# A sink bias added on VectorE, and a normalization issued in two stages, in a two-layer encoder

## What is computed

```
qkv = h @ w_qkv                       # 16 query heads, 4 key/value heads of 64
scores = q k^T / 8 - slope * |t - s|  # only |t - s| <= 128
den = sum exp(scores - m);  lse = m + log(den)
o = (exp(scores - m) @ v) / den
o = o * sigmoid(lse - sink)           # one learned sink logit for each head
x = x + o @ w_out
```

## Time and profile before

| | |
|---|---|
| Runs | 5187.29, 5196.99 and 5769.88 us; median 5196.99 |
| Profiled execution | 5184.39 us; span of its slowest core 5183.3 us |
| Spans of the 8 cores | 5171.3 to 5183.3 us, granted clock 0.932 to 0.936 |
| Busy share of the span | PE 88%, DVE 42%, ACT 27%, POOL 5% |
| DMA | 160.19 MB, mean 31 GB/s |

### The profile page before, as it was taken

How to read it: one execution, slowest core, us unless ns; L and a number is a source line. 1 busy time by engine, 2 the same in 40 slices (tenths; PEclk the granted TensorE clock), 3 DMA queues, 4 the chain that set the end, 5 groups by cost and what they waited for, 6 DMA issues and landing times.

```text
span 5183.3 us, 77281 instructions; the slowest of 8 cores (5171.3 to 5183.3 us)
## 1 busy us (share of the span) xinstructions
PE 4538.4 (88%) x27104; PEld 2251.7 (43%) x27104; DVE 2187.1 (42%) x3136; ACT 1397.6 (27%) x2762; POOL 246.4 (5%) x471
## 2 busy tenths in 40 slices
PE   5767999999999998999767679998999999979996
PEld 2333344455554543444323333443554545434442
DVE  4322322355656565322342233224556565662223
ACT  1574201222232223211215733012132222231112
POOL 0000100000000000000000001000000000000000
PEclk9888899999999998999878889998999999989997
DMA  4100322111111111222221004221111111122211
GB/s 90 25 1 1 56 37 39 21 22 23 21 21 24 19 24 22 41 39 39 58 85 25 1 1 60 37 39 17 26 19 23 21 22 24 23 29 33 39 23 65
DMA packets 85013, 160.19 MB, mean 31 GB/s; under 512 B 8864, under 2 KB 8864, under 8 KB 84640
## 3 DMA queue, kind: packets, MB, share of 16 engines
q0 software_dynamic: 66816, 121.66, 16.5%
q1 hardware_dynamic: 17824, 33.58, 2.1%
HBM read 260.07 MB, written 16.78 MB: 53 GB/s over the span
## 4 chain that ended last, share of the span: by engine, by line
PE 80%; ACT 9%; DVE 5%; issue 4%; DMA 2%; ACTq 0%; DVEq 0%; SPq 0%
PE ps L427 16%; PE ps L464 12%; PE ps L468 12%; PE ps L484 12%; PE ps L716 7%; PE ps L770 5%; PE ps L646 2%; PE ps L767 2%; ACT RD L596 2%; ACT RD L592 2%; PE ps L877 2%; PE ps L603 2%; PE ps L799 2%; PE ps L855 1%; PE ps L403 1%
## 5 line engine op out<-in xcount | busy, mean ns | idle before, releaser
L427 PE MATMUL ps<-A,RING 128*128 128x512 bf16 x3712 | 898.0, 394 | 36.3 <-DVE A L414 20.7
L782 ACT ACTIVATE PT<-ps 128x512 bf16<-128x512 f32 (+3 forms) x864 | 401.2, 467 | 1391.3 <-PE ps L770 1371.5
L464 PE MATMUL ps<-A,RING 128*128 128x512 bf16 x2816 | 670.4, 381 | 0.0
L468 PE MATMUL ps<-A,RING 128*128 128x512 bf16 x2816 | 665.9, 379 | 0.0
L438 DVE TENSOR_TENSOR xT<-ps,xT 128x512 f32<-128x512 f32 x704 | 477.9, 690 | 441.4 <-PE ps L484 341.6
L475 DVE TENSOR_TENSOR SCR<-ps,SG 128x512 bf16<-128x512 f32 x352 | 243.4, 692 | 954.0 <-PE ps L468 954.0
L427 PEld LDWEIGHTS ps<-A,RING 128*128 128x128 bf16 x3712 | 367.9, 101 | 571.0 <-issue 208.3
L484 PE MATMUL ps<-SCR 128*128 128x512 bf16 x2816 | 609.7, 379 | 0.0
L473 ACT ACTIVATE SG<-ps 128x512 bf16<-128x512 f32 x352 | 210.2, 597 | 1404.3 <-PE ps L464 1404.2
L716 PEld LDWEIGHTS ps<-RING,A 128*128 128x128 bf16 x6144 | 394.1, 120 | 69.3 <-issue 49.7
L464 PEld LDWEIGHTS ps<-A,RING 128*128 128x128 bf16 x2816 | 276.7, 98 | 335.3 <-issue 5.6
(11 more groups left out here) (83 smaller groups left out, 3906.3 us busy)
## 6 DMA issues: line engine op xcount, KB each, us to landing
RING<-wts POOLq DMA_DIRECT2D x376, 256.0 KB, 4.5
SCR<-wts POOLq DMA_DIRECT2D x88, 256.0 KB, 10.6
xT<-xin SPq DMA_DIRECT2D x8, 2048.0 KB, 37.7
yout<-SCR SPq DMA_DIRECT2D x64, 256.0 KB, 2.2
GAINS<-gains SPq DMA_DIRECT2D x1, 20.0 KB, 1.8
ESINK<-sink SPq DMA_DIRECT2D x1, 4.0 KB, 5.1
```

The source lines that it names most:

```text
L427: op(PE, lambda kc=kc: nc.tensor.matmul(PS[bank][:, :], slot_proj(s, kc), A[:, kc, tsl], start=(kc == 0), stop=(kc == 7)), reads=[slot_res ...
L464: op(PE, lambda kc=kc: nc.tensor.matmul(PS[bg][:, :], slot_proj(sg_, kc), A[:, kc, tsl], start=(kc == 0), stop=(kc == 7)), reads=[slot_res ...
L468: op(PE, lambda kc=kc: nc.tensor.matmul(PS[bu][:, :], slot_proj(su_, kc), A[:, kc, tsl], start=(kc == 0), stop=(kc == 7)), reads=[slot_res ...
L782: op(ACT, lambda: nc.scalar.activation(out=ptv[:, :, 0:N], in_=psv[:, :, 0:N], func=AF.Exp, scale=0.125), reads=[ps_res[bank]], writes=[pt ...
```

## The change

The eight operations with the bias become additions on DVE, which write den + ESINK into RD. One Ln over all of RD (128x512) on ACT follows. The closure is cut in two, behind the Exp: `normalize` is called at the second item after the group's last (it was the third), `normalize2`, with the SWAP matmul, the copy and the two products, at the fourth. A list `pendq` with counters takes the place of `pend`.

```diff
                         for a in range(4):
                             asl = slice(a * 128, (a + 1) * 128)
-                            op(ACT, lambda a=a, asl=asl: nc.scalar.activation(
-                                out=RD[0:64, asl], in_=PS[db][0:64, asl], func=AF.Ln,
-                                bias=ESINK[0:64, 4 * p + a:4 * p + a + 1], scale=1.0),
+                            op(DVE, lambda a=a, asl=asl: nc.vector.tensor_scalar(
+                                out=RD[0:64, asl], in0=PS[db][0:64, asl], scalar1=ESINK[0:64, 4 * p + a:4 * p + a + 1],
+                                scalar2=None, op0=ALU.add),
                                reads=[ps_res[db]], writes=[rd_res])
...
+                        op(ACT, lambda: nc.scalar.activation(out=RD[:, :], in_=RD[:, :], func=AF.Ln),
+                           reads=[rd_res], writes=[rd_res])
                         op(ACT, lambda: nc.scalar.activation(out=RD[:, :], in_=RD[:, :], func=AF.Exp, scale=-1.0),
                            reads=[rd_res], writes=[rd_res])
+
+                    def normalize2(p=p, b=b, ob=ob, db=db):
+                        tb = b // 4
                         bank = pj_bank()
                         op(PE, lambda: nc.tensor.matmul(PS[bank][:, :], SWAP[:, :], RD[:, :], start=True, stop=True),
                            reads=[rd_res], writes=[ps_res[bank]], sig=True)
...
-                    pend["fn"] = normalize
-                    pend["age"] = 0
-
-            pend = {"fn": None, "age": 0}
+                    pendq.append([2, normalize])
+                    pendq.append([4, normalize2])
+
+            pendq = []
             for i in range(min(LA, n_items)):
                 emit_S(i)
             for i in range(n_items):
                 if i + LA < n_items:
                     emit_S(i + LA)
-                if pend["fn"] is not None:
-                    pend["age"] += 1
-                    if pend["age"] >= 3:
-                        pend["fn"]()
-                        pend["fn"] = None
+                for e_ in pendq:
+                    e_[0] -= 1
+                while pendq and pendq[0][0] <= 0:
+                    pendq.pop(0)[1]()
                 emit_rest(i)
-            if pend["fn"] is not None:
-                pend["fn"]()
-                pend["fn"] = None
+            while pendq:
+                pendq.pop(0)[1]()
```

More of the change, by code:

```diff
@@ L591, in normalize @@
                             asl = slice(a * 128, (a + 1) * 128)
-                            op(ACT, lambda a=a, asl=asl: nc.scalar.activation(
-                                out=RD[0:64, asl], in_=PS[db][0:64, asl], func=AF.Ln,
-                                bias=ESINK[0:64, 4 * p + a:4 * p + a + 1], scale=1.0),
+                            op(DVE, lambda a=a, asl=asl: nc.vector.tensor_scalar(
+                                out=RD[0:64, asl], in0=PS[db][0:64, asl], scalar1=ESINK[0:64, 4 * p + a:4 * p + a + 1],
+                                scalar2=None, op0=ALU.add),
                                reads=[ps_res[db]], writes=[rd_res])
-                            op(ACT, lambda a=a, asl=asl: nc.scalar.activation(
-                                out=RD[64:128, asl], in_=PS[ob][64:128, asl], func=AF.Ln,
-                                bias=ESINK[64:128, 4 * p + a:4 * p + a + 1], scale=1.0),
+                            op(DVE, lambda a=a, asl=asl: nc.vector.tensor_scalar(
+                                out=RD[64:128, asl], in0=PS[ob][64:128, asl],
+                                scalar1=ESINK[64:128, 4 * p + a:4 * p + a + 1], scalar2=None, op0=ALU.add),
                                reads=[ps_res[ob]], writes=[rd_res])
+                        op(ACT, lambda: nc.scalar.activation(out=RD[:, :], in_=RD[:, :], func=AF.Ln),
+                           reads=[rd_res], writes=[rd_res])
                         op(ACT, lambda: nc.scalar.activation(out=RD[:, :], in_=RD[:, :], func=AF.Exp, scale=-1.0),
                            reads=[rd_res], writes=[rd_res])
+                    def normalize2(p=p, b=b, ob=ob, db=db):
+                        tb = b // 4
                         bank = pj_bank()
```

## The result

The changed kernel takes 5374.39 us in the median of its runs, its profiled execution 5373.89 where the kernel before had 5184.39: 189.5 us more. The ratio is 1.0358, with a 95% interval of 1.0344 to 1.0371: slower.

The account below looks back on a forecast made before the run. PE (88% busy) was taken to bound most of the kernel, but no engine layer 0's attention. A 10.63 us ring plus 1.4 for low clock gave 12.03 a group, +167 on 5184.4: 5350 us, range 5270 to 5430.

Parts of the forecast that it names:

- a ring through PE, DVE and ACT: Layer 0's attention: SWAP, copy, products, adds, Ln, Exp, two tiles, back to SWAP; 10.63 us at full clock; chance 0.70.
- what the low clock costs a group: TensorE at 1.2 GHz in the burst behind PE's wait: 1.4 us taken of a possible 2.2 to 2.6.
- the full-clock group of before: One attention group of the kernel before, at full clock: 8.11 us, where 9.31 was read from the profile.
- The price of an add: Each 64x128 DVE add from PSUM: 0.345 us long, one every 0.45, so 3.60 for eight.
- Ln and Exp: ACT's term between the eighth add and the next exponential: 1.38 us together.
- What the adds wait for: DVE's adds queue behind the former group's copy and two products, free 3.65 us after SWAP, not behind PE.
- Both PE terms of the ring: SWAP to copy, 1.27 us, and two tiles of PE work, 1.31; at 1.2 GHz 2.22 and 2.56.
- The sum: Layer 0's attention: 30 intervals at 12.03 us plus first and last group, 83.6 more a sequence, +167 for two.
- All else is as before: Feed-forward, layer 1, weight DMAs and SP's transfers were to stay unchanged, with no new DMA.
- B: Rival in layer 0's attention: the ring with cheap adds or a recovering clock, 5210 to 5294 us; chance 0.16.
- C: Rival in layer 0's attention: adds hide beside the tiles' work, groups of 6.4 us, 5013 in all; chance 0.04.
- D: Rival in layer 0's attention: clock stays low through the burst, groups of 13.3 us, 5428 in all; chance 0.10.

Follow-up runs that it names:

- e4: Changed kernel plus 22 idle matmuls of 128x512 behind each first stage, in PE's wait; 5260.1 us in one run.
- e10: Kernel before the change plus 12 idle matmuls of 128x512 ahead of each SWAP product; 5105 to 5108 us, ratio 0.9846.
- e3: Changed kernel with two RD buffers used in turn instead of one; 5367.5 us in one run.
- e5: Changed kernel, both stages kept, with two adds of 64x512 against a spread exp(sink) table for the eight; 5255.1 us on the slowest core, 5208 compared.
- e1: Kernel before with the eight adds on DVE and one Ln and Exp, but one stage at the third tile; 5241.3 us in one run.
- e11: e1 plus 12 idle matmuls of 128x512 ahead of each SWAP product; 5147 to 5195 us, ratio 0.9944 to the kernel before.
- e7: Kernel before with exp(sink) added by a TensorE identity matmul, two Ln of 64x512, no adds, one stage; 4980.3 to 4981.6 us, ratio 0.9603.
- e8: As e7, but SWAP, copy and products a tile later, at the fourth, with two RD buffers; 5005.2 and 5006.0 us, ratio 0.9651.

## Why the prediction was right or wrong, and the step that failed

The mechanism held: a ring through PE, DVE and ACT, closed by program order. The step that failed is one term of the sum, what the low clock costs a group, taken at 1.4 and measured at 1.9. That the whole came out only 22.5 us above the forecast is in part luck.

**The bound and the ring: right, and shown.** The full-clock ring is 10.51 (e4) for 10.63, the full-clock group of before 8.11 (e10) as worked out. Of the 3.12 a group that the change costs (12.43 for 9.31), 2.40 is structure, and 0.7 is that the clock costs more than before.

**The price of an add: right.** 0.342 and 0.356 measured (L592, L596) for 0.345, start to start 0.454 for 0.45. The estimate from the Trainium skill, "VectorE: DVE Perf Modes", the section on the TRN2 errata, 0.26, was too low by 0.08 to 0.1. The 0.05 for the per-partition operand, read off from L414 against L438, is about half of that.

**Ln and Exp:** 1.26 for 1.38. Ln to Exp 0.72 as taken; Exp to the next exponential 0.54, not 0.66.

**What the adds wait for: right.** DVE's own order, not RD (e3) and not PE. That the adds take as long on DVE as the eight Ln on ACT, and save nothing, stands too: they are 3.63 of the ring, and two in their place gave about 165 us back (e5).

**The clock: the step that failed, by its size.** The prediction had 2.2 to 2.6 from its own rows and took 1.4. Measured are 12.43 - 10.54 = 1.9 on average, and 2.1 in the commonest group of 12.60 (2.52 for 1.31 and 2.08 for 1.19). With Ln and Exp 0.1 shorter, a group is 12.43 for 12.03.

The 1.4 was scaled from the kernel before, where the fall meets only part of the burst. There SWAP stands right behind PE's wait of 3.1 us, and in 20 of the 32 groups of the first sequence it took 1.10 to 1.16 us, the full clock; it took 2.04 in two. The low clock came only behind it (411.74 to 413.02). In the kernel after the wait is 5.3 us, the first value product behind it already takes 0.59 for 0.38, and SWAP took 1.91 in 20 of 32 groups. Both PE terms of the ring lie at this head of the burst. I had the row-based 2.2 and did not trust it.

**The sum.** It had 83.6 us more a sequence (a stretch of "about 385"); the stretch grew by 97.1. The 13.5 missing are 30 x 0.40 = 12 for the groups, 0.65 for the last interval (9.85 for 9.2) and 0.9 for the first group (2.9 for 2). Two sequences make 27. "All else is as before" did not hold to the microsecond either: the input was there 8.8 us sooner, which hid a third of the miss, and 4 us came elsewhere. 27 - 8.8 + 4 is the 22.5 between 167 and 189.5.

**The rivals.** B and C ask for shorter adds or a cover that is not there; the first is measured away, the second needs ACT to have no wait before Ln, and it waits 4.9. D (13.3) was half right: of its 2.6 the 2.2 of the two terms fell due nearly whole. The other 0.4 would have needed PE's path at low clock to outlast DVE's, and the low clock ends inside the burst, behind SWAP (the four mask matmuls at 443.16 take 0.45 together, those at 440.18 took 0.63, those at 443.88 take 0.39). The rule of the Trainium skill ("ScalarE: Activation LUTs", rules for kernel authors) that an add belongs on VectorE brought nothing here: 0.342 to 0.356 on DVE, 0.36 on ACT, at 128 columns of float32 from PSUM. Its figure is for bf16; the adds here are float32.

**An error of mine in an expectation:** that one stage leaves the ring open (e1). e11 showed a ring of 8.79.

What stays open: why the low clock comes at once behind one wait and later behind the other was not tested by itself, and neither was what sets the input's arrival.

## What to carry to other kernels

Before moving work to an engine with room, walk the ring: from the operation's result through every engine back to its own queue. An engine's busy share (22% here) says nothing about where its queue stands in that ring, and a later stage for the consumer makes the ring longer, not shorter, when the producer's next turn is queued behind that consumer.

Count instructions, not elements: eight small operations cost the same 3.6 us on either engine, two large ones 1.6, and on TensorE, as one more term of a sum that was there anyway, 0.4.

When PE waits a few microseconds in each turn of a loop, price the chain twice, at both clocks. For what stands right behind the wait, do not carry the cost over from a loop with a shorter wait: behind 3.1 us it was mostly full clock here, behind 5.3 us mostly low. Idle matmuls in the wait are a cheap experiment that separates structure from clock.

Read what a change did from marks inside the trace on both sides of it, and not from the total alone: 9 us of the input's arrival hid part of the loss here.

## What the runs showed of the hardware

- Idle matmuls in a wait paid for themselves: 22 of them a group gave 114 us (e4, clock 0.77 to 1.00), 12 gave 80 us in the kernel before (e10, 0.86 to 1.00).
- From the kernel before to e1, PE's wait at SWAP went from 3.1 us to 3.6 to 3.9, the clock from 0.86 to 0.83, and the clock's part of a group from 1.1 or 1.2 to 1.4. SWAP right behind the wait took 2.04 us in 2 of 32 groups before and in 25 of 32 in e1. With waits of 0.6 and 1.2 us (e7, e8) the clock was 1.00.
- Ln of 64x512 from PSUM took 0.58 to 0.59 (e7), from SBUF 0.626.
- The first use of the input waited for its DMA until 43.7 us in the trace of the kernel before and until 34.6 in that of the kernel after, though nothing ahead of it differs. A total of one kernel against another holds such a difference.
